# A fused two-model kernel: block changes, constant products and the order of VectorE's weight splits

## What is computed

```python
# first model
h = h + sgu_mixer(rms_norm(h))                 # gelu, spatial gating in blocks of 128
h = h + conv_ffn(rms_norm(h))                  # up to 2*2816, causal conv of 3, silu gate, down
h = h + rwkv7_mixer(rms_norm(h))               # r, k, v, low-rank rates, wkv7 scan, gate, w_o
h = h + conv_ffn(rms_norm(h))
h = rms_norm(h)
# second model
x = x + even_mixer(rms_norm(x))    # w_in gives q, k, v, z, xbc, dt: neighbourhood attention
                                   # on q, k, v; a two-way SSD scan gated by z; then w_out
x = x + swiglu_ffn(rms_norm(x))
x = x + odd_mixer(rms_norm(x))     # qkv, rope, grouped attention, w_out
x = x + swiglu_ffn(rms_norm(x))
```

## Time and profile before

| | us |
|---|---|
| median of three runs | 2829.59 (2829.07 to 2830.23) |
| the profiled execution | 2831.85 |
| its span, first to last instruction | 2830.0 |
| busy: PE / DVE / ACT / POOL | 2746.4 / 1524.7 / 1051.5 / 789.3 |
| granted TensorE clock, mean over the span | 0.991 of 2.4 GHz |

### The profile page before, as it was taken

How to read it: one execution, slowest core, us unless ns; L and a number is a source line. 1 busy time by engine, 2 the same in 40 slices (tenths; PEclk the granted TensorE clock), 3 DMA queues, 4 the chain that set the end, 5 groups by cost and what they waited for, 6 DMA issues and landing times. The chain is left out here.

```text
span 2830.0 us, 38120 instructions
## 1 busy us (share of the span) xinstructions
PE 2746.4 (97%) x14012; PEld 2174.5 (77%) x14012; DVE 1524.7 (54%) x1928; ACT 1051.5 (37%) x1869; POOL 789.3 (28%) x718
## 2 busy tenths in 40 slices
PE   8999999999999999999999998999999999999999
PEld 6888888657898788888777765788888656788887
DVE  4477762554756677754467655544443256644432
ACT  5433332334445333333245534322222257322221
POOL 3231111450825421112103545311112045311100
PEclk9999999999999999999999999999999999999999
DMA  4222223311100123223221121222233210222333
GB/s 151 76 96 96 96 89 97 99 53 60 53 2 20 45 97 96 96 86 99 78 82 61 36 63 30 82 97 96 96 89 97 90 38 2 68 97 96 96 93 101
DMA packets 80543, 219.01 MB, mean 77 GB/s; under 512 B 21917, under 2 KB 22045, under 8 KB 80158
## 3 DMA queue, kind: packets, MB, share of 16 engines
q1 hardware_dynamic: 79262, 215.17, 24.3%
q10 hardware_dynamic: 1152, 2.10, 0.2%
HBM read 215.14 MB, written 2.10 MB: 77 GB/s over the span
## 5 line engine op out<-in xcount | busy, mean ns | idle before, releaser
L311 PE MATMUL psum<-rounded,high_r 128*128 128x512 f32 x3040 | 1199.4, 395 | 18.9 <-DVE rounded L390 9.9
L315 PE MATMUL psum<-rounded,ring_low 128*128 128x512 f32 x3040 | 1186.3, 390 | 0.0
L313 PE MATMUL psum<-rounded,high_r 128*128 128x512 f32 x3040 | 1186.3, 390 | 0.0
L336 ACT ACTIVATE high_r<-ring 128x1024 fp32r<-128x1024 f32 (+2 forms) x432 | 420.3, 973 | 1403.9 <-PE psum L315 1381.5
L341 DVE TENSOR_TENSOR ring_low<-ring,high_r 128x1024 fp32r<-128x1024 f32 (+2 forms) x432 | 526.3, 1218 | 565.0 <-ACT high_r L336 563.7
L311 PEld LDWEIGHTS psum<-rounded,high_r 128*128 128x128 f32 x3040 | 572.3, 188 | 171.8 <-issue 23.9
L315 PEld LDWEIGHTS psum<-rounded,ring_low 128*128 128x128 f32 x3040 | 572.3, 188 | 120.5
L313 PEld LDWEIGHTS psum<-rounded,high_r 128*128 128x128 f32 x3040 | 572.4, 188 | 117.6 <-issue 1.7
L774 DVE TENSOR_TENSOR arena<-psum,inverse 128x512 f32<-128x512 f32 x176 | 121.5, 691 | 314.5 <-PE psum L315 314.4
L629 POOL CAST rounded<-rows 128x512 f32 (+1 forms) x88 | 53.9, 613 | 785.5 <-DVE rows L779 785.5
L631 POOL TENSOR_TENSOR rounded<-rows,rounded 128x512 f32 (+1 forms) x88 | 115.5, 1313 | 13.2 <-POOL rounded L629 11.9
(11 more groups left out here) (416 smaller groups left out, 2899.8 us busy)
## 6 DMA issues: line engine op xcount, KB each, us to landing
ring<-in_up SPq DMA_DIRECT2D x176, 512.0 KB, 3.4
ring<-in_down SPq DMA_DIRECT2D x64, 384.0 KB, 3.1
ring<-in_down SPq DMA_DIRECT2D x64, 320.0 KB, 2.9
ring<-in_even_in SPq DMA_DIRECT2D x36, 512.0 KB, 3.3
ring<-in_sgu_in SPq DMA_DIRECT2D x16, 512.0 KB, 3.5
ring<-in_even_out SPq DMA_DIRECT2D x16, 384.0 KB, 3.1
ring<-in_qkv SPq DMA_DIRECT2D x12, 512.0 KB, 3.2
ring<-in_sgu_out SPq DMA_DIRECT2D x8, 512.0 KB, 3.4
```

Source lines behind the costliest of these rows:

```text
L311: nc.tensor.matmul(psum[:, m, :], high_r[:, r % HIGHS, blk], x_high, start=(k0 + k == 0), stop=False)
L313: nc.tensor.matmul(psum[:, m, :], high_r[:, r % HIGHS, blk], x_low, start=False, stop=False)
L315: mm = nc.tensor.matmul(psum[:, m, :], ring_low[:, r % R, blk], x_high, start=False, stop=end)
L336: nc.scalar.activation(high_r[:, r % HIGHS, 0:nk * P], ring[:, r % R, 0:nk * P], ACT.Copy).then_inc(unit_high, 1)
```

## The change

Four edits.

1. *Fewer constants multiplied.* 55 of the 79 stand-ins go: at the start of the rwkv block (4 and 13), of the even block (10) and of the qkv block (8), before the output turn of rwkv (4), before the even mixer's rates (1), and in steps 6, 10 and 14 of the attention (5 each). Those of the scan, of step 2 and of the wkv7 part stay (24).
2. *Unit 1's split behind the block change.* For `rwkv_k`, `even_in` and `qkv` (`SPLIT_SECOND`), ScalarE's and VectorE's splits of unit 1 leave the tail of the matrix before and stand at the start of `split_and_read` of the new one (for qkv, ahead of its loop).
3. *The last addition of squares behind the block change.* GpSimd squares the last tile but does not add it; VectorE does so as its first work in the even block (two additions) and in the qkv block (one). A new semaphore, `last_summed`, lets TensorE's sum over ones and ScalarE's start wait for it.
4. *Gate tiles.* For tiles 28 to 35 VectorE's split of unit n + 2 stands behind `read` and `side` (the steps) of tile n. ScalarE's order stays.

```diff
+        SPLIT_SECOND = ("rwkv_k", "even_in", "qkv")
...
+            def split_two_behind(g, r):
+                if not (isinstance(g, int) and g == st.groups - 1 and r + 2 >= st.body):
+                    split(eng, st, g, r + 2)
+                elif following and following not in SPLIT_LATE and not (r + 1 == st.body and following in SPLIT_SECOND):
+                    split(eng, Stream(following), 0, r + 2 - st.body)
...
-                    if not (isinstance(g, int) and g == st.groups - 1 and r + 2 >= st.body):
-                        split(eng, st, g, r + 2)
-                    elif following and following not in SPLIT_LATE:
-                        split(eng, Stream(following), 0, r + 2 - st.body)
+                    behind = split_last and split_last(g * st.body + r)
+                    if not behind:
+                        split_two_behind(g, r)
...
                         side(g * st.body + r)
+                    if behind:
+                        split_two_behind(g, r)
             if name in SPLIT_LATE and name not in SPLIT_BEFORE:
                 split(eng, st, 0, 0)
+                split(eng, st, 0, 1)
+            if name in SPLIT_SECOND:
                 split(eng, st, 0, 1)
...
-                if i:
+                if i and (add_last or i < tiles - 1):
...
                     nc.gpsimd.tensor_tensor(square, x, x, ALU.mult).then_inc(squared, 1)
+                    if i == KD - 1:
+                        return
...
-                    occupy(3, 4)
                     nc.tensor.matmul(psum[:, 4, :], con("ones"), square_sum[:, :], start=True, stop=False)
                     pe.wait_ge(last_squared, 1)
                     nc.tensor.matmul(psum[:, 4, :], con("ones"), inverse[:, 1, :], start=False, stop=True).then_inc(totalled, 1)
-                    occupy(3, 13)
...
                         if i == 0:
-                            occupy(4, 4)
                             pe.wait_ge(applied, 1)
...
                     def totals():
+                        pe.wait_ge(last_summed, 2)
...
-                            if i in (6, 10, 14):
-                                occupy(2, 5)
...
                             totals()
-                            occupy(3, 1)
                             rates()
...
-                    occupy(3, 10)
                     products(pe, name, x_parts, scaled, after_unit=beside, bank_of=bank_of)
...
-                    split_and_read(dve, name, split_low, read, early=scale, after_first=start, side=beside)
+                    nc.vector.tensor_tensor(square_sum[:, :], square_sum[:, :], arena[:, ZS + 1, :], ALU.add).then_inc(last_summed, 1)
+                    nc.vector.tensor_tensor(shrink[:, :], shrink[:, :], arena[:, SQUARES + 1, :], ALU.add).then_inc(last_summed, 1)
+                    split_and_read(dve, name, split_low, read, early=scale, after_first=start, side=beside, split_last=lambda n: n >= GATES)
...
-                    occupy(3, 8)
                     products(pe, name, two_parts(XH, XL), scaled, after_unit=beside, bank_of=bank_of)
...
+                    nc.vector.tensor_tensor(square_sum[:, :], square_sum[:, :], arena[:, SQUARES + 1, :], ALU.add).then_inc(last_summed, 1)
+                    next_split(dve, split_low, 1)
                     for n in range(TILES):
                         next_split(dve, split_low, n + 2)
```

More of the change, by code:

```diff
@@ L100, in build @@
             "cleared_before", "dt_loaded", "dt_high_done", "dt_low_done", "totalled", "guarded", "rooted", "inverted", "first_inverted",
-            "scaled", "biased", "tap0", "tap1", "tap3", "dt_done", "dt_scaled")]
+            "scaled", "biased", "tap0", "tap1", "tap3", "dt_done", "dt_scaled", "last_summed")]
         bias_loaded = whole.enter_context(nc.semaphore("bias_loaded"))
@@ L342, in split_low, with split_and_read @@
                                     high_r[:, r % HIGHS, 0:nk * P].bitcast(F32), ALU.subtract).then_inc(unit_low, 1)
-        def split_and_read(eng, name, split, read=None, inputs=None, early=None, after_first=None, side=None):
+        def split_and_read(eng, name, split, read=None, inputs=None, early=None, after_first=None, side=None, split_last=None):
             st = Stream(name)
             following = (ORDER + [None])[ORDER.index(name) + 1]
+            def split_two_behind(g, r):
[3 more added lines that the diff above has]
+                    split(eng, Stream(following), 0, r + 2 - st.body)
             def body(g):
@@ L417, in add_low, with sum_squares @@
             split_and_read(dve, name, split_low, read if handed else None, inputs=inputs, early=add)
-        def sum_squares(pool, taken, squared, squares_summed, tiles=KD):
+        def sum_squares(pool, taken, squared, squares_summed, tiles=KD, add_last=True):
             for i in range(tiles):
@@ L721, in _ @@
                         pool.wait_ge(totalled, 1)
-                        sum_squares(pool, taken, squared, summed, KD - 1 if layer == 0 else KD)
+                        sum_squares(pool, taken, squared, summed, KD - 1 if layer == 0 else KD, layer != 2)
                 @block.scalar
@@ L2199, in even @@
             (cleared_before, dt_loaded, dt_high_done, dt_low_done, totalled, guarded, rooted, inverted, first_inverted,
-             scaled, biased, tap0, tap1, tap3, dt_done, dt_scaled) = even_early
+             scaled, biased, tap0, tap1, tap3, dt_done, dt_scaled, last_summed) = even_early
             with phase("silu_done", "normed", "dt_turned", "dt_kept", "abs_done", "exp_done", "ln_done", "gains_done", "dt_ready",
@@ L2551, in start @@
                         act.wait_ge(dt_loaded, 16)
+                        act.wait_ge(last_summed, 2)
                         nc.scalar.activation(dt_high, dt_raw, ACT.Copy).then_inc(dt_high_done, 1)
@@ L3079, in turn_bank @@
                 return 5 + s % 3 if s < FIRST else 7
-            (cleared_before, _, _, _, totalled, _, rooted, inverted, _, scaled, *_) = even_early
+            (cleared_before, _, _, _, totalled, _, rooted, inverted, _, scaled, *_, last_summed) = even_early
             with phase("rope_loaded", "squared", "gathered", "head_rooted", "head_inverted", "head_spread", "head_scaled", "rotated",
@@ L3142, in beside @@
                         if n == 0:
+                            pe.wait_ge(last_summed, 3)
                             nc.tensor.matmul(psum[:, 4, :], con("ones"), square_sum[:, :], start=True, stop=True).then_inc(totalled, 1)
@@ L3269, in step @@
                             nc.scalar.activation(x, x, ACT.Copy, scale=one(rc, i - 1, 1)).then_inc(second_normed, 1)
+                    next_split(act, split_high, 1)
                     for n in range(TILES):
```

## The result

The median is **2794.77 us** of 4 runs (2792.18 to 2797.10); the kernel before, run beside it, took 2829.91 (2829.07 to 2830.36). The ratio is 0.9874, with a 95% interval of 0.9862 to 0.9886. The forecast was 2795.5, in a range of 2786 to 2807. The profiled execution took 2794.94 (span 2793.1), against 2831.85 (span 2830.0) before: 36.9 less, where the sum said 34.1.

A forecast was written before the change was run, and what follows sets the result against it. TensorE, busy for 97% of the span, was taken as the bound. Terms of +1.9, -1.3, -7.9, -6.0 and -20.8 sum to -34.1 us: 2831.85 to 2797.8 profiled, 2795.5 on the median's footing; range 2786 to 2807.

The forecast's parts named there:

- Into rwkv: Start of the rwkv block: opening 1.7 us earlier, and 3.4 gained at the sums without four stand-ins.
- The stall on `ring_low`: Before rwkv's unit 1: TensorE waits for VectorE's split, now behind three mixes; 5.3 us lost.
- rival 3: At rwkv's unit 1: its split is ready in time, no new wait; -7.0, 2788.5 us; chance 0.05.
- The clock behind it: After the stall in rwkv: one stretch at half clock, 1.7 us lost, bounds 0 and 3.4.
- Output turn: In rwkv: L1546 no longer behind four stand-ins, waits only for GpSimd's L2082; 1.3 us gained, at least 0.
- Into even: Start of the even block: 3.2 us from earlier opening, 6.4 from ten stand-ins, less 1.7 of clock; 7.9 gained.
- Into qkv: Start of the qkv block: 2.1 us from earlier opening, 5.6 from stand-ins, less 1.7 of clock; 6.0 gained.
- Attention: Beside the gate tiles: 5.5, 6.8 and 5.3 us at tiles 31, 33, 35, other waits 4.0, less 0.8 clock; 20.8 gained.
- Dearer clock: Two half-clock stretches at each of three block changes, one at each of three attention stalls; +9.4, 2805 us; chance 0.12.
- The split's move buys nothing: Attention: something else releases the steps, so only stand-ins go, 11.3 us instead of 21.6; 2806 us; chance 0.09.
- No new rwkv wait: At rwkv's unit 1: the split is ready in time; -7.0, 2788.5 us; chance 0.05.
- The clock does not return: Attention: clock drops at tile 29's steps and stays low until the attention ends; +43.7, 2839 us; chance 0.03.

The follow-up runs named there:

- the fastest kernel: The changed kernel with VectorE's split of unit 1 in the rwkv block made before the first low-rank mixes instead of behind them; 2789.25 us, ratio 0.9858.
- the last experiment: The fastest kernel with ScalarE's split of weights also behind its attention steps, at the odd gate tiles (29, 31, 33, 35) alone; 2791.99 us, ratio 0.9858.

## Why the prediction was right

**The sum held because its terms did**, the larger part of them within 0.3 us. Two gains were forecast 1.6 and 2.0 too small, and one loss 1.1 too small:

- *Into rwkv*, 5.1 for opening and sums: 5.1. Waits in the chain of the first unit's products could be followed in the trace of before, and nothing else was late. The 3.4 for the sums was put down to the four stand-ins alone, though, and half of it was clock: they and the sums ran at 0.69 behind a gap of 2.74; with the stand-ins back behind a gap of 1.06 it was 1.00 and they cost 1.7, and with the gap of 2.74 back the sums ran at 0.53 without them. The total was right because both went.
- *The stall on `ring_low`*, 5.3: 5.0 to 5.2. It was found in the order of the code and priced by the earlier trace rows; without it the forecast would have been rival 3's. The experiment that takes it away shows the price from the other side, 4.8.
- *The clock behind it*, 1.7: mis-sized, it was 2.8, within the bound of 3.4. The kernels with the stall filled (5.67 for the unit) and with the stall away (5.49) show that this was clock.
- *Output turn*, 1.3: 1.3, but in part by luck. L1555 did not wait for GpSimd, whose addition (L2091) ends only at 940.09 by the profile, where spans on GpSimd are rough. It started at 939.62, as soon as TensorE's work ahead of it ended, 1.8 earlier than before; the later turns gave 0.5 of that back.
- *Into even*, 7.9: 9.9. The term of one fall of the clock, 1.7, did not come: the granted clock was 1.00 behind a gap of 2.72. The fall of the earlier trace rows had followed a gap of 6.07, and with such a gap put back it came again. The other 0.3 are the low part, 0.88 for 1.0, and roundings. *Into qkv*, 6.0: 6.3; there the fall came and cost 1.5.
- *Attention*, 20.8: 22.4. The odd tiles came as forecast (5.5, 6.8, 5.3), half-clock stand-ins included, since both were read off the same rows. The rest was 4.8 for 4.0. The clock was on the wrong side of the sum: I took 0.8 off for a new fall, while before stood at 0.95 there and after at 1.00, so falls went away. The wait for the windows ended at 2.2, not under 2.
- *Down0*, nothing: 2.4, which is a stretch at half clock that one profiled execution had and the other had not. It cancels against 1.4 and 1.0 lost in the wkv part and the scan, so the touched places gained 37.0, and the forecast was 2.9 short there. The medians are 35.1 apart. That the forecast came within 0.7 of the new median is partly luck: stretches of this kind come and go, and the four runs of after lie 4.9 apart.

Two slips in the working change nothing: "the rest of rows 7" is read from the earlier trace rows, and the span of "my case alone" by its own bounds (5.1 of clock either way, 4.0 between 0 and 5.3) is 2789 to 2805, not to 2802.

**The rivals.** *Dearer clock*: out. The mean granted clock of the profiled executions was 0.991 before and 0.993 after, although 55 of the 79 products that were there to keep it up had gone. Of the three stretches taken, unit 1 of rwkv and unit 0 of qkv had a fall, unit 0 of even had none, and the attention had 1.00. *The split's move buys nothing*: out by 11.3 us. *No new rwkv wait*: out by 5.01. *The clock does not return*: out; the attention ran at 1.00, and unit 1 of rwkv, the longest case, had full clock back before its end (0.52 from 551 to 557, 1.00 from 559.34 to 562). The experiment without the last 24 is where this rival's mechanism shows at last, at 3.3 us and in another stage, the scan.

**What the whole is worth by part**: stand-ins 18.4, VectorE's order 11.3, block changes 1.0 (an opening of 3.3, 5.8 into even and some 2 into qkv against a stall of 8.0 are 3), together 30.6 before rounding; the difference is 35.1. They need not add up, since each is what its edits are worth last. The 3.2 us of the attention that either of two edits brings alone are in none of them. Some 2 us into even are in two (6.0 for the stand-ins, 5.8 for the block change, 9.9 for both), as each run with one of them undone has its own fall of the clock there. The rest is within the spread of the runs.

## What to carry to other kernels

A product that only keeps the clock up can be worth having in a long thin stretch (24 of them: 3.3 us), and where it stands in time that the engine would spend waiting in any case (2.7 us at the one place tried, not to be seen in the median). Ahead of a product whose inputs are ready, or behind the wait that it should bridge, it costs its whole length (55 of them, 13 of which filled a wait: 18.4 us), where a fall of the clock behind a gap cost 1.5 to 2.8. Two changes at one place can overlap: what each is worth alone and what each is worth last differ, here by 3.2 us. When work is moved behind something on an in-order queue, list what was behind it *and* what now stands ahead of it: VectorE's split behind the attention steps won 11, the same split behind three mixes lost 8, and ScalarE's behind its steps lost 14, since VectorE's next work waited for it. Then look for the nearest place at which the engine idles anyway: one split moved there gave 5.5 more.

## What the runs showed of the hardware

- Gaps of the same length had different results, and each the same one every time: 2.72 idle into even was followed by a granted clock of 1.00 and 2.72 into qkv by 0.70, and in eight traces the 24 products behind them took 5.5 to 5.6 and 7.1 to 7.2 us. Behind 6.06 into even they took 8.1. What decides between even and qkv stays open.
- A fall needs no long stop: in the scan of the kernel without stand-ins the clock is 0.96 over 224 us with TensorE busy for 213.57 of them, and its longest listed wait there is 1.6 us.
- Falls also come and go at places that an edit does not touch (20 to 50: 0.94 before, 1.00 after). The runs of one kernel spread: 1.3 to 2.8 us before and 1.0 in the fastest kernel, but 4.9 after, 6.2 with the 55 stand-ins back, 7.8 in the last experiment and 9.0 with the block changes back; the number of stand-ins does not order them. The clock goes with it: in the last experiment the run of 2786.26 had a mean of 0.995, the two of 2794.0 had 0.991. A gain of 2 us at a place, shown by the trace, need not be seen in the median.
- VectorE's low part took 0.88 where GpSimd was busy for only its first 0.3, 1.74 beside a GpSimd addition. In the fastest kernel a split took 1.78 at 544.27 and 1.21 at 550.74, both beside GpSimd, whose shifts took 2.03 and 2.00 there, against 1.04 for the one at 547.12. So the two engines slow each other in some of these pairs; which one pays, and when, isn't settled here. Moving GpSimd's two additions into even to VectorE (0.69 and 0.68) so gave VectorE back 0.86 at its low part.
